# The last adaptive tiles of a block move from ahead of the scan into the heads of its second stream

## What is computed

```python
sh1, sc1, gt1, sh2, sc2, gt2 = ada_mod(c, w_ada[l], b_ada[l], 6)     # silu(c) @ w_ada + b_ada, cut in six
...
hx = modulate(rms_norm(h_x, g_mix[l]), sh1, sc1)
u, gate, z, xbc, dt_raw = split_proj(hx @ p["w_in"])
xs, bm, cm, dt = ssd_scan_inputs(xbc, dt_raw, p)
h_x = h_x + gt1 * mixer_output(u, gate, z, xs, bm, cm, dt, a, hf0, hb0, p, rows)
h_x = h_x + gt2 * hier_moe(modulate(rms_norm(h_x, g_ffn[l]), sh2, sc2), p)
```

## Time and profile before

| what | value |
|---|---|
| median of 3 runs | 2552.22 us (2548.83 to 2563.39) |
| profiled execution | 2556.97 us, of which the span of the trace is 2555.3 us |
| PE busy | 2199.8 us (86%) |
| PEld busy | 1933.2 us (76%) |
| DVE busy | 1588.1 us (62%) |
| ACT busy | 1111.8 us (44%) |
| POOL busy | 474.7 us (19%) |
| mean granted TensorE clock | 0.927 of full |
| memory traffic | 471.50 MB, mean 185 GB/s |

### The profile page before, as it was taken

One profiled execution on the slowest core, in us unless ns is written; L12 is line 12 of the kernel. 1 busy time (PEld: TensorE's weight loads), 2 busy tenths in 40 slices (PEclk: granted clock), 3 DMA queues, 4 the chain that ended last, 5 costly groups with the idle time before them and its releaser, 6 DMA issues.

```text
span 2555.3 us, 40376 instructions
## 1 busy us (share of the span) xinstructions
PE 2199.8 (86%) x15366; PEld 1933.2 (76%) x15376; DVE 1588.1 (62%) x2534; ACT 1111.8 (44%) x1624; POOL 474.7 (19%) x328
## 2 busy tenths in 40 slices
PE   5999887688589775876889999889997999899997
PEld 2776565677377565765868999779996999878997
DVE  2876654477468455765555776576667666546665
ACT  3223443576433544674445455224332433445332
POOL 1000001688400015884052021100000000000000
PEclk7998997899789887998999999989998999999999
DMA  6458611799445036996424466455553345323452
GB/s 249 165 205 320 216 58 63 274 344 347 181 148 199 32 116 215 326 322 223 134 98 181 167 217 225 158 196 188 184 186 132 139 174 205 132 100 116 173 186 85
DMA packets 103174, 471.50 MB, mean 185 GB/s; under 512 B 11520, under 2 KB 30208, under 8 KB 66048
## 3 DMA queue, kind: packets, MB, share of 16 engines
q1 hardware_dynamic: 84480, 404.79, 44.7%
q0 software_dynamic: 13232, 44.84, 4.7%
q10 hardware_dynamic: 5328, 20.07, 1.9%
HBM read 412.76 MB, written 54.79 MB: 183 GB/s over the span
## 4 chain that ended last, share of the span: by engine, by line
PE 42%; DVE 6%; ACT 2%; issue 1%; DVEq 1%; SPq 1%; DMA 0%; POOL 0%; ACTq 0%; POOLq 0%
PE bank L749 12%; PE bank L751 12%; PE bank L750 12%; DVE ring_halves L419 2%; ACT high L1402 1%; PE bank L1257 1%; PE bank L1121 1%; PE bank L1234 1%; PE bank L1247 1%; PE bank L1309 1%; PE bank L1290 1%; PE bank L1239 1%; PE bank L800 0%; DVE dring_halves L428 0%; PE bank L1238 0%
## 5 line engine op out<-in xcount | busy, mean ns | idle before, releaser
L749 PE MATMUL bank<-ssdb_halves,high 128*128 128x256 f32 (+1 forms) x2080 | 620.8, 298 | 49.1 <-DVE HT_halves L1934 18.4
L750 PE MATMUL bank<-HT_halves,high 128*128 128x256 f32 (+1 forms) x2096 | 621.9, 297 | 0.0
L751 PE MATMUL bank<-ssdb_halves,ring_halves 128*128 128x256 f32 (+1 forms) x2080 | 618.4, 297 | 0.0
L419 DVE TENSOR_TENSOR ring_halves<-ring,high 128x2048 fp32r<-128x2048 f32 (+1 forms) x230 | 482.3, 2098 | 195.9 <-ACT high L1402 194.3
L1402 ACT CAST high<-ring 128x2048 fp32r<-128x2048 f32 x230 | 437.3, 1903 | 218.5 <-PE bank L751 120.9
L749 PEld LDWEIGHTS bank<-ssdb_halves,high 128*128 128x128 f32 x2080 | 397.8, 191 | 68.6 <-issue 37.7
L750 PEld LDWEIGHTS bank<-HT_halves,high 128*128 128x128 f32 x2096 | 403.3, 192 | 8.9
L751 PEld LDWEIGHTS bank<-ssdb_halves,ring_halves 128*128 128x128 f32 x2080 | 398.2, 191 | 10.1
L419 POOL TENSOR_TENSOR ring_halves<-ring,high 128x1024 fp32r<-128x1024 f32 x66 | 224.7, 3405 | 674.9 <-ACT high L1402 674.9
L428 DVE TENSOR_TENSOR dring_halves<-dring,dhigh 128x1024 fp32r<-128x1024 f32 (+1 forms) x152 | 226.2, 1488 | 160.8 <-ACT dhigh L1408 160.3
L1408 ACT CAST dhigh<-dring 128x1024 fp32r<-128x1024 f32 x152 | 160.4, 1056 | 244.7 <-PE bank L751 244.6
(11 more groups left out here) (440 smaller groups left out, 3970.3 us busy)
## 6 DMA issues: line engine op xcount, KB each, us to landing
ring<-in_ffn SPq DMA_DIRECT2D x88, 1024.0 KB, 5.6
ring<-in_moe SPq DMA_DIRECT2D x64, 1024.0 KB, 7.3
ring<-in_ada SPq DMA_DIRECT2D x48, 1024.0 KB, 6.1
dring<-in_ffn_down SPq DMA_DIRECT2D x88, 512.0 KB, 3.6
dring<-in_moe_down SPq DMA_DIRECT2D x64, 512.0 KB, 4.6
ring<-in_foxin SPq DMA_DIRECT2D x24, 1024.0 KB, 4.9
ring<-in_win SPq DMA_DIRECT2D x22, 1024.0 KB, 8.0
zs_b<-x_slots POOLq DMA_DIRECT2D x32, 512.0 KB, 8.6
```

What stands on the lines that cost most here:

```text
L419: eng.tensor_tensor(low, w, h, ALU.subtract).then_inc(sem(f"low_{engine}"), 1)
L749: mm(o, a[0], b[0], start=first, stop=last and bool(kw), **kw)
L750: mm(o, a[0], b[1], start=False, stop=last and bool(kw), **kw)
L751: return mm(o, a[1], b[0], start=False, stop=last, **kw)
```

## The change

The last 8 tiles of part 1 and the last 4 of part 2 (`ADA_HEADS = (8, 4)`) are no longer multiplied in the tail. Each is multiplied behind one head's output in the scan's stream 0, one per head, from head 0 on. Their rows are turned two tiles later instead of one (`lag=2`), the last two behind the loop. ScalarE copies each row behind the exponentials of the head two further on; in block 0 the last two copies stand behind the loop. VectorE's additions are cut in two: the first part still ahead of the scan, the second ahead of the residuals, and TensorE waits for that one ahead of the second norm's mean. The mean of the scan's norm moves to another bank. In block 0 ScalarE's three late copies are gone (`ADA_SILU`), and the step sizes are turned ahead of all the tail.

```diff
@@ -141,7 +141,7 @@
 RAW = ("ada", "poolw", "s5tab")
 ADA_AHEAD = (0, 2)
 ADA_BETWEEN = ([0, 2, 2, 2, 2, 2, 2, 2, 2, 2, 0], [0, 0, 0, 0, 2, 2, 2, 0, 0, 0, 0])
-ADA_SILU = 3
+ADA_HEADS = (8, 4)
 CONV_STEPS = ([10, 6, 6, 6, 7, 6, 6, 7, 8], [0, 3, 3, 3, 10, 12, 3, 2, 0])
 LOW_BOTH = ("rt", "moe", "over")
 
@@ -762,7 +762,7 @@
                 o = 4 * j + 2 * c if q < ADA_FIRST else 48 * l + 4 * (j // 2) + 2 * c
                 return (ps[2] if q < ADA_FIRST else ps[6 + q % 2])[:, o:o + 2]
 
-            def ada_tile(part, q):
+            def ada_tile(part, q, lag=1):
 
                 tiles = ADA_PARTS[part]
                 t = TILES_OF["ada", part][q - tiles[0]]
@@ -770,6 +770,8 @@
                 w = ring[t % RING][:].rearrange("p (a b) -> p a b", a=KC)
                 if q >= 2:
                     pe.wait_ge(*at("ada_row", q - 2))
+                if lag == 2 and q - 2 >= tiles[-1] + 1 - ADA_HEADS[part - 1]:
+                    ada_turned(q - 2)
                 if part and q in (tiles[0], tiles[0] + 1):
                     pe.wait_ge(*at("root", ("mix", part - 1)))
                 for c in range(KC):
@@ -780,7 +782,7 @@
                         i.then_inc(sem("ada_sums"), 1)
                 pe.wait_ge(sem("ada_sums"), 4 * (q + 1))
                 pe.drain().then_inc(sem("tile_free"), 1)
-                if q > tiles[0]:
+                if lag == 1 and q > tiles[0]:
                     ada_turned(q - 1)
 
             def ada(part, first, count):
@@ -789,7 +791,7 @@
                     ada_tile(part, q)
                     if q == ADA_FIRST - 2:
                         mean_square(("mix", 0), slice(0, 2 * T))
-                if first + count == ADA_PARTS[part][-1] + 1:
+                if first + count == ada_end(part):
                     ada_turned(first + count - 1)
 
             def mean_square(n, tok):
@@ -879,9 +881,8 @@
                 for j in (18, 19, 15, 16, 17):
                     pe.wait_ge(*at(*win_taken(l, j)))
                 mean4(("ln_mean", l), lambda c: MIX[:, c, tok], 4, tok, lambda c: at("conv_y", l))
-                ada(l + 1, q0, 1)
                 narrow_turned(("win", l), 16, 3, 0, 2 * TB).then_inc(*done("dt_raw", l))
-                ada(l + 1, q0 + 1, ADA_PARTS[l + 1][-1] - q0)
+                ada(l + 1, q0, ada_end(l + 1) - q0)
 
             def ssd(l, s, full):
                 o = s * T
@@ -975,6 +976,11 @@
                     if h + 2 < HEADS:
                         decay(h + 2)
                     outputs(h)
+                    if s == 0 and h < ADA_HEADS[l]:
+                        ada_tile(l + 1, ada_end(l + 1) + h, 2)
+                if s == 0:
+                    for q in (ADA_PARTS[l + 1][-1] - 1, ADA_PARTS[l + 1][-1]):
+                        ada_turned(q)
 
             def mean4(name, src, bank, tok, ready):
 
@@ -1359,8 +1365,9 @@
                 ssd(l, 1, not last)
                 pe.wait_ge(*at("h0", (l, 1)))
                 ssd(l, 0, True)
-                mean4(("ssd_ms", l), lambda c: sq[:, 4 + c, tok], 6, tok, lambda c: at("ssd_sq", l))
+                mean4(("ssd_ms", l), lambda c: sq[:, 4 + c, tok], 4, tok, lambda c: at("ssd_sq", l))
                 wout(l, tok)
+                pe.wait_ge(*at("s5_dve", ("ada_heads", l + 1)))
                 mean_square(("ffn", l), tok)
                 router(l, 2 if last else 4)
                 moe(l, TB if last else 2 * TB)
@@ -1484,21 +1491,19 @@
                         q += ADA_BETWEEN[l][j // 2]
                     if j % 2 and j // 2 + 2 < WIN_TILES:
                         make_high(SPLIT_AT["win", l] + j // 2 + 2)
-                end = ADA_PARTS[l + 1][-1] + 1
                 if l:
                     ssd_in(l, 0)
                     narrow(("win", l), ps[len(W_IN_ORDER) % 6], 16, 2 * T)
-                    ada(l + 1, q, end - q)
+                    ada(l + 1, q, ada_end(l + 1) - q)
                     ssd_in(l, 1)
                     ln_squares(l)
                     softplus_log("dt", l, dts[:, 3, :, :], dts[:, 1, :, :])
                 else:
                     narrow(("win", l), ps[len(W_IN_ORDER) % 6], 16, 2 * T)
-                    ada(l + 1, q, end - ADA_SILU - q)
+                    ada(l + 1, q, ada_end(l + 1) - q)
                     ssd_in(l, 0)
                     ln_squares(l)
                     softplus_log("dt", l, dts[:, 3, :, :], dts[:, 1, :, :])
-                    ada(l + 1, end - ADA_SILU, ADA_SILU)
                     ssd_in(l, 1)
 
             def softplus_log(name, key, e, src):
@@ -1570,13 +1575,17 @@
                         i = act_fn(off_b[:, p, :].rearrange("p (a c) -> p a c", a=2),
                                    b[:].rearrange("p (a m c) -> p a m c", a=2, m=2)[:, :, 1, :], ACT.Exp)
                     i.then_inc(*done("decayed", (l, s, h)))
+                    if s == 0 and 2 <= h < ADA_HEADS[l] + 2:
+                        ada(l + 1, ada_end(l + 1) + h - 2, 1)
+                if s == 0 and ADA_HEADS[l] > HEADS - 2:
+                    ada(l + 1, ADA_PARTS[l + 1][-1] - 1, 2)
 
             def mixer_norms(l, tok):
                 act.wait_ge(*at("y_done", l))
                 act_fn(sq[:, 4:8, tok], MIX[:, 4:8, tok], ACT.Square).then_inc(*done("ssd_sq", l))
                 ln_silu(l, tok.stop)
                 act.wait_ge(*at("mean4", ("ssd_ms", l)))
-                act_fn(rms[:, tok], ps[6][:, tok], ACT.Sqrt, bias=k("eps6")).then_inc(*done("ssd_root", l))
+                act_fn(rms[:, tok], ps[4][:, tok], ACT.Sqrt, bias=k("eps6")).then_inc(*done("ssd_root", l))
                 act.drain()
                 for c in range(KC):
                     if c >= 4:
@@ -1894,9 +1903,8 @@
             dve.wait_ge(sem("vec_loaded"), 32)
             dve.wait_ge(sem("x_loaded"), 16)
 
-            def ada(part):
-
-                tiles = ADA_PARTS[part]
+            def ada(part, tiles, key="ada"):
+
                 dve.wait_ge(*at("ada_turned", tiles[-1]))
                 vectors = [(q // ADA_TILES, q % ADA_TILES // (D // TCOLS)) for q in tiles[::D // TCOLS]]
                 for l in sorted({a for a, _ in vectors}):
@@ -1911,7 +1919,7 @@
                         turned = ps[6 + h][:, 48 * l + x.start:48 * l + x.stop].rearrange("p (i a) -> p i a", a=4)
                         i = tt(own_half(mod[l]), turned, own_half(v(f"b_ada{l}")), ALU.add)
                 if part:
-                    i.then_inc(*done("s5_dve", ("ada", part)))
+                    i.then_inc(*done("s5_dve", (key, part)))
                 dve.drain()
                 for l, i in vectors:
                     if i % 3 == 1:
@@ -2687,7 +2695,7 @@
                         then(j - 1)
                 then(KC - 1)
 
-            ada(0)
+            ada(0, ADA_PARTS[0])
             for l in range(DEPTH):
                 last = l == DEPTH - 1
                 streams = 1 if last else 2
@@ -2712,10 +2720,11 @@
                     for _ in sconv(l, 1):
                         pass
                 steps(l)
-                ada(l + 1)
+                ada(l + 1, range(ADA_PARTS[l + 1][0], ada_end(l + 1)))
                 ssd(l, 1, not last)
                 ssd(l, 0, True)
                 mixer_norms(l, tok)
+                ada(l + 1, range(ada_end(l + 1), ADA_PARTS[l + 1][-1] + 1), "ada_heads")
                 residual(("wout", l), [0, 1, 2, 3], lambda j, s: mod[l][:, 16 + j, s:s + 1], streams)
                 dve.drain()
                 scale(("ffn", l), streams, lambda c, s: gsc[l][:, 1, c, s:s + 1], bias(1), MIX_r)
@@ -2754,6 +2763,11 @@
             dve.drain().then_inc(*done("x_ready", "end"))
 
     return seen
+
+
+def ada_end(part):
+
+    return ADA_PARTS[part][-1] + 1 - (ADA_HEADS[part - 1] if part else 0)
 
 
 def win_taken(l, j):
```

## The result

The changed kernel took 2559.98 us (median of 20 runs, 2548.29 to 2565.17), the kernel before 2552.18 (20 runs, 2543.75 to 2563.39) on the same chips: a ratio of 1.0025, 95% interval 1.0013 to 1.0036. A second comparison, made at the end of the study, gave 2556.50 against 2554.13, 1.0008 [0.9991, 1.0024]. By the ratios the change costs 6.4 us (3 to 9) in the first comparison and 2.0 us (a gain of 2 to a loss of 6) in the second; the medians differ by 7.8 and 2.4. All of it is within 0.5%, and the forecast was +6.2.

What follows compares the result with a forecast made beforehand. TensorE was taken to bound the heads, with mixed bounds ahead of the scan. Block 0 (-8.2 + 11.6 + 4.75 = +8.2) and block 1 (-8.6 + 6.6 = -2.0) gave +6.2 on 2552.22: 2558.5 us, range 2545 to 2577 (8 in 10).

Steps and rivals of the forecast that it cites:

- Start of block 0's scan: Ahead of block 0's scan: TensorE starts it at 235.5 instead of 243.72, 8.2 us gained.
- Heads of block 0: Scan heads of block 0, stream s = 0: the eight moved tiles cost TensorE 11.6 us, between 10 and 14.
- End of the scan: Behind block 0's last head: a turn, tile, copy and two casts precede ScalarE's square, 4.75 us lost.
- some 1.5 more: End of block 0's scan: extra loss if TensorE's clock is low for the mean, some 1.5 us.
- All behind it is a chain, so the loss stays: Behind block 0's square: Silu, root, reciprocal and splits form a chain headed by ScalarE, so the 4.75 us loss stays.
- Block 1: Block 1: 8.6 us gained ahead of the scan, 6.6 us lost in its heads, together -2.0 us.
- Clears: SP's queue: 32 slot clears ahead of the router's tile, issued from about 335.5 to 381, cost 0 with 5 us margin.
- Sum: Whole kernel: block 0 +8.2 and block 1 -2.0, together +6.2 us.
- (1) The clock in the heads: Rival, heads with tiles: TensorE's clock falls to half, +18 to +36 us on the forecast, 2576 to 2594; chance 0.14.
- (2) The clears: Rival, SP's queue: clears hold up the router and expert tiles; a 60 us clearing costs some 9 us, 2567; chance 0.08.
- (3) Heads that hide the tiles: Rival, scan heads: tiles cost nothing there, leaving -16.8 + 4.75 = -12 us, 2540; chance 0.06.
- (4) The repeated turns: Block 1: row 43 turned five times, not once, 2.1 us of TensorE, covered: 0, at most 2; no separate chance given.

Runs made afterwards that it cites:

- casts_first: The changed kernel, but ScalarE makes each output-projection cast in the wait for one of block 0's last two tiles: 2551.08 us, 0.9999 of the kernel before.
- b1_only: The change in block 1 only (`ADA_HEADS = (0, 4)`), block 0 as before: 2549.96 us, 0.9988 of the kernel before.
- b0_only: The change in block 0 only (`ADA_HEADS = (8, 0)`), block 1 as before: 2561.19 us, 1.0034 of the kernel before.
- six_four: The changed kernel with `ADA_HEADS = (6, 4)`, four tiles staying in block 0's tail, no repeated turns: 2549.96 us, 0.9989 of the kernel before.
- more_clears: The changed kernel with 16 more 512 KB transfers of zeros behind the 32 clears: 2572.11 us, 1.0069 of the kernel before.
- two_two: The changed kernel with `ADA_HEADS = (2, 2)`, the tail's last two rows copied behind ScalarE's logarithm: 2547.06 us, 0.9978 of the kernel before; again 2545.24, 0.9974.
- two_two_warm: The (2, 2) kernel plus unread products ahead of the second score group, the norm's mean and the output projection: 2543.92 us, 0.9973 of the kernel before.

## Why the prediction was right

The forecast of +6.2 us and "same" was met, and by most of its own steps. That the medians come so near to it (+7.8 and +2.4) is in part luck: one term was left out, and one came out better.

- **Start of block 0's scan** (235.5, 8.2 gained): 235.99 and 235.30, so 7.7 and 8.4. The 14 us of idle time came; the trace names ScalarE's Silu group as what ended it, not VectorE's additions, which end at the same time.
- **Heads of block 0** (11.6): from the first output product to the end of the last, 25.2 us before (304.35 to 329.55), 36.0 after: 10.8. The tile without a turn costs 1.28, with it 1.81, as taken from the tail, and the tiles of heads 5 and 6 together 2.8, as forecast. Off was only the 0.1 for each entry: it is 0 (the 0.22 us note is in the 1.29).
- **End of the scan** (4.75): 5.6 - 1.15 = 4.45. casts_first took the order away, and 3.6 to 4.0 us with it. The prediction's "some 1.5 more" for a low clock at the mean is no part of the change: it comes and goes with the execution. ScalarE's root waited 0.41 us for a mean of 5.84 us in the first profile of after, not at all for one of 5.46 in the second, and 1.22 us for one of 6.66 in b1_only, whose block 0 is that of before:

```profile
332.67 3.70 PE L983 MATMUL bank<-wide,con 128*128 128x512 f32 x8 [3.13 <-ACT wide L1576]
...
331.45 6.66 PE L992 MATMUL bank<-wide,con 128*128 128x512 f32 x8 [3.13 <-ACT wide L1590]
...
338.15 0.69 ACT L1593 ACTIVATE rms<-bank,con 128x512 f32<-128x512 f32 x1 [1.22 <-PE bank L992]
```

  (the first line is of before, the others of b1_only).
- **"All behind it is a chain, so the loss stays"**: it stays. C-B grew by 15.7 against before, and D-C is 1.4 to 1.6 us shorter in the two profiles of after than in that of before; but b1_only, with the same block 0 as before, has the shortest of all, 84.37. The starts of the output projection's second group, 5.14 us behind C in after and 5.26 in before, give only 0.1 of the difference. The mean granted clock from C to D was 0.87 in before, 0.90 in after and 0.93 in b1_only. So D-C differs from one execution to the next (in these three it is longer where the clock was lower), and no run shows that the change moves it.
- **A term that was missing: the clock at the scan's start.** The prediction counts 14 us of idle time as free. Six profiles start the scan at 235 to 237 us without a fill: B-A was 53.0 us in five of them (the second of after, b0_only, casts_first, six_four, more_clears) and 48.63 in one. With block 0 as before it was 51.39 and 48.69. The means are 52.3 and 50.0: some 2 us, which the prediction put at nothing. Two profiles on one side are too few to say more.
- **Block 1** (-8.6 + 6.6 = -2.0): E-D -8.8, with the repeated turns in it; F-E +5.0, since the four tiles cost 6.2 (start of the stream's first to its last output product) but the stretch ahead of them takes 1.2 less, for a reason that was not looked for. Sum -3.8, and b1_only alone -4.0, better than forecast.
- **Clears** (0, with 5 us of margin): 0. They were issued from 332.0 and not 335.5, and ended at 375.2 and not 381. The margin's size was wrong both ways: nothing at the router's cast, some 7.5 us at the expert's, which is the one that counts.
- **Sum.** Against the single profile of before, D is at +3.6 and +7.1 and block 1 at -3.8 and -4.3: -0.2 and +2.9 in the two profiles. b0_only and b1_only give more executions of each block. The mean D of the three with block 0 as in after (434.20, 437.70, 438.36) is 7.8 us behind that of the two with block 0 as before (430.60, 427.28): A -8.7, B-A +1.5, C-B +14.9, D-C +0.1. For block 1, E-D + F-E has a mean of 470.4 in three and of 474.1 in two: -3.7. Forecast were +8.2 and -2.0. The sum of +4.1 lies between the two measurements, 6.4 and 2.0 by the ratios. With profiles that differ by several us for one program, the last 2 us either way stay open.
- **Two slips in the working**, with no effect on the forecast: bounds of -2 to +12 put on 2552.2 give 2550 to 2564, not 2549 to 2566; and the chances of the two rivals sum to about 0.17 for "slower", not 0.16.

**Rivals.** (1) The clock in the heads: refuted, 1.00 in every window of the heads with tiles. But the clock did act, at a place that the prediction had not priced: the scan's start, behind the idle time that the change makes. The Trainium skill, page "TensorE: Matmul & The Clock Gate", Part 1, says that the slow state is the default and sustained activity releases it; both profiles agree in that the scan starts at 0.50 behind 14 us of idle time and rises under work. (2) The clears: no cost with 32, 14.2 us with 48. (3) Heads that hide the tiles: refuted, 5.00 and 5.52 us a head where it was 3.72. (4) The repeated turns: seen, in block 1's projection. b1_only, which has none, has E-D of 400.46 beside 400.70 and 400.33, so they cost nothing that can be told.

## What to carry to other kernels

Moving work out of a wait is worth the wait only up to what is next late. Here the scan of block 0 started 4.6 us earlier with two tiles in the heads (and late copies), 4.7 with four, 7.0 with six and 7.7 with eight, while each tile cost its full 1.3 to 1.8 us in heads that TensorE bounded: the last two bought 0.7 us for 3.6. Find that point and move only so many. two_two was the only choice clearly better than before, but it also copies its last rows later and moves only two tiles in block 1, so how much of its gain is the number of tiles was not measured apart. And look at what the move does to the order on the engine that serves it: two casts behind a copy instead of ahead of it cost as much as two tiles.

Before filling idle time to keep TensorE warm, look at what covers the cold work: a cold mean beside ScalarE's Silu and a cold first group beside VectorE's splitting cost next to nothing here, and the fill only moved the cold stretch to where it did cost.

## What the hardware showed

- The same program, with nearly the same idle time ahead (14.26 and 13.87 us), raised TensorE's clock from 1.2 to 2.4 GHz 3.4 us into the work in one execution and 10.5 us in another: 48.63 and 53.03 us for one stretch. two_two, two_two again and two_two_warm, alike until just ahead of B, gave 53.02, 53.06 and 48.37. The difference is there by the first output product of the stream with s = 1: 22.95 and 27.22 us behind A in the two profiles of after, 27.01, 26.77 and 22.70 in those three. One profile of each can't tell two kernels apart by 5 us here.
- Tiles of 32 rows, one in each head among products of 128 rows, left the clock at 1.00. In the tail of before, eight of them in a row, parted by turns, it fell to 0.50.
- A mean of 5.1 to 5.5 us on a cold TensorE instead of 3.70 cost nothing (two_two, casts_first, the second profile of after), since ScalarE's Silu lies beside it; one of 6.66 cost 1.22 (b1_only).
